# Up projection of a float32 encoder kernel: hi and lo tokens in one 512-column matmul per weight block

## The chip, the core and the metric

The kernel runs on one core of a Trainium2 chip. Engines named here: TensorE (PE in the profile; its weight loads are PEld), VectorE (DVE), ScalarE (ACT), GpSimd (POOL) and SyncE (SP), which issues the transfers. The metric is device time in microseconds (us), the median of several runs; lower is better.

## What is computed

Two layers over 256 tokens of width 2048, all in float32. Each layer is attention with three head groups and then a squared-ReLU MLP. What matters here is the MLP, whose hidden width is 8192:

```python
for l in range(DEPTH):                      # DEPTH = 2
    h = rmsnorm(x, norm1_g[l])
    proj = h @ w_in[l]
    ...                                     # three attention mixers -> mixed
    x = x + mixed @ w_out[l]
    h2 = rmsnorm(x, norm2_g[l])
    x = x + jnp.square(jax.nn.relu(h2 @ w_up[l])) @ w_down[l]
```

## The kernel before

**Three passes for float32.** Every operand of a projection is split in two: `hi`, a copy rounded to the type float32r, and `lo`, the remainder `value - hi`. A product is the sum of three matmuls: hi x hi, hi x lo and lo x hi. The tokens are kept transposed in `xt` (a hi and a lo tensor, each `[128, 16, 256]`: 16 blocks of 128 input features, 256 tokens). Weights arrive as *units* of 256 rows x 512 columns (512 KB) in `raw_ring` (8 slots). ScalarE casts a unit to `w_hi` (`split_hi`, L604), VectorE subtracts for `w_lo` (`split_lo`, L776); both have `AHEAD = 4` slots. So unit s+4 is cast once unit s has been used, and TensorE comes to it three units later.

**Order of the work.** Each engine runs one list of steps, one per unit, written out by hand in `layer_steps`: 72 units of `w_in` (with attention in between), 32 of `w_out`, then the MLP. The MLP alternates an *up stage* of 32 units (4 chunks of 512 hidden columns, 8 units each) and a *down stage* of 32 units (8 chunks, 4 units each), four times per layer, so 8 up stages and 8 down stages in all. Engines meet only at semaphores; every engine works through its list in order.

**Up chunk** (`up_unit`, L447). Weights are stationary and tokens move: for each of the unit's 2 row blocks `j` and 4 column blocks `f`, three matmuls of 256 columns (L460 `w_hi` with `xt` hi, L461 `w_hi` with `xt` lo, L462 `w_lo` with `xt` hi) add into the same half of an accumulator bank of `acc`. Each matmul has a weight load of its own. A chunk takes two whole banks, `acc[2p]` and `acc[2p+1]`, p being the chunk's parity. ScalarE then reads both with a Relu into `mlp_t` (L717), after its `split_hi` of that step, and increments `evicted[p]`; VectorE squares `mlp_t` in the next step (L1018), ScalarE casts the result to `ht` hi (L723), VectorE forms `ht` lo (L1024).

**Down, in and out chunks** (`rows_unit`, L431, with `three_passes`, L419). Here 128 tokens are stationary and 512 weight columns move: L421, L422, L423. Down chunks are read by VectorE (L1009).

**Accumulator banks.** There are eight of 512 float32 columns: `acc` (4), `ps_s` (attention scores and part of the first chunk), `ps_p` (transposed probabilities, the same), `ps_v` (attention values), `ps_t` (transposes). TensorE waits for `evicted[p]` before a chunk's first unit, that is for the reading of the chunk two earlier.

**Around the first up stage.** The second norm's transposed tokens are still being made: TensorE transposes x into `ps_t` (L468) after steps 104 + 1 and 104 + 2, VectorE reads it (L822), ScalarE and VectorE split it (L617, L834), and the units of the first up chunk wait for their block (`panel_done`).

Of the kernel before, what the change touches and what calls it, by code (L numbers as in the profile page):

```python
# [28 lines left out]
P = 128  # L29
# [119 lines left out]
def encoder(nc, x_in, norm1_g, w_in, a_qnorm_g, a_knorm_g, a_rel_bias, b_qnorm_g, b_knorm_g, b_sinks, c_qnorm_g,  # L149
            c_knorm_g, c_lambda_q1, c_lambda_k1, c_lambda_q2, c_lambda_k2, c_subln_g, w_out, norm2_g, w_up, w_down,  # L150
            consts, out):
    with ExitStack() as ctx:
        def sb(name, shape, dt=F32):
            return ctx.enter_context(nc.sbuf_tensor(name, shape, dt))
# [6 lines left out]
        xt = [sb(f"xt_{h}", [P, KT, SEQ], F32R) for h in ("hi", "lo")]  # L161
# [32 lines left out]
        acc = ctx.enter_context(nc.psum_tensor("acc", [P, 4, CW], F32))  # L194
        ps_s = ctx.enter_context(nc.psum_tensor("ps_s", [P, CW], F32))
        ps_p = ctx.enter_context(nc.psum_tensor("ps_p", [P, CW], F32))
        ps_v = ctx.enter_context(nc.psum_tensor("ps_v", [P, CW], F32))
        ps_t = ctx.enter_context(nc.psum_tensor("ps_t", [P, CW], F32))
# [10 lines left out]


# [24 lines left out]
        rstd_ready = sem("rstd_ready")  # L235
        relu2 = sem("relu2")
# [181 lines left out]
        def _(pe):  # L418
# [28 lines left out]
            def up_unit(pl, u, k, chunk):  # L447

                slot, p = u % AHEAD, chunk % 2
                if k == 0:  # L450
                    pe.wait_ge(evicted[p], pl.evictions(chunk))
                unit_is_split(pl, u)
                for j in range(2):
                    for f in range(4):
                        o = acc[:, 2 * p + f // 2, (f % 2) * SEQ:(f % 2 + 1) * SEQ]
                        hi, lo = (w[:, slot, j, f * P:(f + 1) * P] for w in (w_hi, w_lo))
                        kt = 2 * k + j
                        last = k == UPC - 1 and j == 1

                        pe.matmul(o, hi, xt[0][:, kt, :], start=kt == 0 and f % 2 == 0, stop=False, skip_group_check=True)  # L460
                        pe.matmul(o, hi, xt[1][:, kt, :], start=False, stop=False, skip_group_check=True)  # L461
                        mm = pe.matmul(o, lo, xt[0][:, kt, :], start=False, stop=last, skip_group_check=True)  # L462
                mm.then_inc(unit_done, 1)
# [106 lines left out]
            def mlp(pl, s, part, buf, c, k, n):  # L570
                if part == "up":
                    if s < LOOP0 and c == 0:
                        pe.wait_ge(panel_done, pl.at(PANELS, PANELS_BEFORE + FIRST_X2 + k + 1))
                    up_unit(pl, s, k, n)
                else:
                    if k == 0 and c % 4 == 0:

                        done = (4 if s >= DOWN3 else 0) + 2 * (buf + 1) + (8 if s >= DOWN3 else 0)
                        pe.wait_ge(h_done, pl.at(H_CHUNKS, done, 4))
                    rows_unit(pl, s, ht, (8 * buf + 2 * k, 8 * buf + 2 * k + 1), n, k == 0, k == 3, CW)  # L580
                if s in T_USE:
                    use_t(pl, s)
# [17 lines left out]
        def _(act):  # L600
# [112 lines left out]
            def activations(pl, s, part, c, k, n):  # L713

                if part == "up" and k == UPC - 1:
                    act.wait_ge(unit_done, pl.unit(s + 1 + AHEAD))
                    act.activation(mlp_t[c % 2][:, :], acc[:, 2 * (n % 2):2 * (n % 2) + 2, :].rearrange("p b n -> p (b n)"),  # L717
                                   ACT.Relu).then_inc(evicted[n % 2], 1)
# [46 lines left out]
        def _(dve):  # L765
# [228 lines left out]
            def mlp(pl, s, part, buf, c, k, n):  # L994
# [16 lines left out]
                if s == UNITS - 1:  # L1011
                    split_lo(pl, s + AHEAD)
                late = late_chunk(s, part, c, k, 0)
                if late is not None:
# [3 lines left out]
                    dve.tensor_tensor(mlp_t[q % 2][:, :], mlp_t[q % 2][:, :], mlp_t[q % 2][:, :], ALU.mult).then_inc(relu2, 1)  # L1018
# [162 lines left out]
```

## Time and profile before

| | |
|---|---|
| median of 3 runs | 2197.22 us (2193.01 to 2197.33) |
| the profiled execution | 2191.94 us |
| its span, first to last instruction | 2190.1 us |
| mean granted TensorE clock over the span | 0.997 |
| TensorE matmul busy | 98% |
| TensorE weight load busy | 87% |
| VectorE busy | 59% |
| ScalarE busy | 45% |
| GpSimd busy | 9% |

The span is what the trace covers; 1.84 us of the execution lie around it. A matmul's duration in the trace reaches from its start to the end of its passage through the array, so durations of neighbouring matmuls overlap and their sum is more than the time that they take. What one costs in a row of them is the distance from one start to the next.

### The profile page before, as it was taken

To read this page: it belongs to the slowest core of one execution; us is meant where nothing else is said; L and a number is where in the kernel's file an instruction comes from. 1 tells how busy PE (TensorE), PEld (TensorE's weight loads), DVE (VectorE), ACT (ScalarE), POOL (GpSimd) and SP (SyncE) were. 2 spreads that over 40 slices of the span, in tenths; PEclk is the share of its full clock that TensorE was granted. 3 is DMA by queue.
4 is the path that set the end of the run, shared out by engine and by line. 5 is a ranking of instruction groups with operands and counts; after the bars stand their busy time and mean duration, and the time that the engine had idled before them with its cause. 6 is when DMAs were issued, how large, how long until landed. Compare 5 with 4: busy or idle time off the path is not lost.

```text
span 2190.1 us, 31018 instructions
## 1 busy us (share of the span) xinstructions
PE 2154.4 (98%) x12790; PEld 1895.0 (87%) x12790; DVE 1301.6 (59%) x1737; ACT 989.5 (45%) x1357; POOL 196.7 (9%) x170
## 2 busy tenths in 40 slices
PE   8999999999999999999999999999999999999999
PEld 6777888998998998899878777889989989988987
DVE  7778546555556555555677775465555555555556
ACT  5545544443344344344445455444434433443444
POOL 3223230000000000000022322200000000000000
PEclk9999999999999999999999999999999999999999
DMA  8553336656655655665556533466566556556554
GB/s 268 157 177 107 118 132 184 182 184 194 188 185 193 187 184 190 192 183 191 183 163 184 150 97 125 144 176 181 191 193 184 184 194 190 183 192 190 184 187 151
DMA packets 203756, 384.45 MB, mean 176 GB/s; under 512 B 13310, under 2 KB 20192, under 8 KB 203616
## 3 DMA queue, kind: packets, MB, share of 16 engines
q1 hardware_dynamic: 202816, 382.11, 56.1%
q8 instruction: 101, 1.65, 0.3%
q10 hardware_dynamic: 800, 0.37, 0.1%
q14 instruction: 39, 0.32, 0.0%
HBM read 380.31 MB, written 2.12 MB: 175 GB/s over the span
## 4 chain that ended last, share of the span: by engine, by line
PE 91%; DVE 6%; ACT 1%; SPq 1%; issue 0%; DMA 0%; DVEq 0%; ACTq 0%
PE acc L421 17%; PE acc L423 17%; PE acc L422 17%; PE acc L462 11%; PE acc L461 11%; PE acc L460 11%; DVE w_lo L776 3%; PE ps_t L468 2%; PE ps_s L519 1%; PE ps_s L518 1%; PE ps_p L533 1%; PE ps_v L549 1%; PE ps_v L550 1%; ACT w_hi L604 1%; DVE small L795 0%
## 5 line engine op out<-in xcount | busy, mean ns | idle before, releaser
L776 DVE TENSOR_TENSOR w_lo<-raw_ring,w_hi 128x1024 fp32r<-128x1024 f32 (+1 forms) x690 | 851.4, 1235 | 791.1 <-ACT w_hi L604 789.8
L604 ACT CAST w_hi<-raw_ring 128x1024 fp32r<-128x1024 f32 (+1 forms) x724 | 751.6, 1038 | 988.1 <-PE acc L423 567.6
L460 PE MATMUL acc<-xt_hi,w_hi 128*128 128x256 f32 x2048 | 580.6, 283 | 0.0
L462 PE MATMUL acc<-xt_hi,w_lo 128*128 128x256 f32 x2048 | 580.3, 283 | 0.0
L461 PE MATMUL acc<-xt_lo,w_hi 128*128 128x256 f32 x2048 | 580.3, 283 | 0.0
L421 PE MATMUL acc<-w_hi,ht_hi 128*128 128x512 f32 x1280 | 503.2, 393 | 0.0
L423 PE MATMUL acc<-w_hi,ht_lo 128*128 128x512 f32 x1280 | 499.1, 390 | 0.0
L422 PE MATMUL acc<-w_lo,ht_hi 128*128 128x512 f32 x1280 | 498.7, 390 | 0.0
L460 PEld LDWEIGHTS acc<-xt_hi,w_hi 128*128 128x128 f32 x2048 | 393.5, 192 | 0.3
L461 PEld LDWEIGHTS acc<-xt_lo,w_hi 128*128 128x128 f32 x2048 | 393.5, 192 | 0.3
L462 PEld LDWEIGHTS acc<-xt_hi,w_lo 128*128 128x128 f32 x2048 | 393.4, 192 | 0.0
L421 PEld LDWEIGHTS acc<-w_hi,ht_hi 128*128 128x128 f32 x1280 | 240.4, 188 | 52.2 <-issue 3.3
L423 PEld LDWEIGHTS acc<-w_hi,ht_lo 128*128 128x128 f32 x1280 | 240.3, 188 | 50.6
L422 PEld LDWEIGHTS acc<-w_lo,ht_hi 128*128 128x128 f32 x1280 | 240.6, 188 | 48.4
L421 PE MATMUL acc<-w_hi,xt_hi 128*128 128x512 f32 (+1 forms) x512 | 203.0, 397 | 0.0
L423 PE MATMUL acc<-w_hi,xt_lo 128*128 128x512 f32 (+1 forms) x512 | 195.5, 382 | 0.0
L422 PE MATMUL acc<-w_lo,xt_hi 128*128 128x512 f32 (+1 forms) x512 | 194.8, 381 | 0.0
L421 PEld LDWEIGHTS acc<-w_hi,xt_hi 128*128 128x128 f32 x512 | 97.7, 191 | 27.1 <-issue 10.9
L423 PEld LDWEIGHTS acc<-w_hi,xt_lo 128*128 128x128 f32 x512 | 97.5, 191 | 19.1
L422 PEld LDWEIGHTS acc<-w_lo,xt_hi 128*128 128x128 f32 x512 | 97.9, 191 | 15.8
L1125 POOL TENSOR_TENSOR head_sq<-head_in,rope_s 128x256 f32<-128x256 f32 (+1 forms) x20 | 15.0, 752 | 975.9 <-DVE small L857 975.9
L1140 POOL TENSOR_TENSOR w_lo<-raw_ring,w_hi 128x1024 fp32r<-128x1024 f32 x34 | 81.9, 2408 | 214.4 <-ACT w_hi L604 214.4
(141 smaller groups left out, 1372.2 us busy)
## 6 DMA issues: line engine op xcount, KB each, us to landing
raw_ring<-in_w_up_dram SPq DMA_DIRECT2D x256, 512.0 KB, 3.7
raw_ring<-in_w_down_dram SPq DMA_DIRECT2D x256, 512.0 KB, 3.6
raw_ring<-in_w_in_dram SPq DMA_DIRECT2D x132, 512.0 KB, 3.9
raw_ring<-in_w_out_dram SPq DMA_DIRECT2D x64, 512.0 KB, 3.6
raw_ring<-in_w_in_dram SPq DMA_DIRECT2D x16, 256.0 KB, 2.8
x<-in_x_dram SPq DMA_DIRECT2D x4, 512.0 KB, 8.8
out_dram<-x SPq DMA_DIRECT2D x4, 512.0 KB, 3.9
bias_t<-ext_bias SPq DMA_DIRECT2D x2, 512.0 KB, 8.1
```

The source lines that it names most:

```text
L421: pe.matmul(out_ap, t_hi, m_hi, start=start, stop=False, skip_group_check=True)
L422: pe.matmul(out_ap, t_hi, m_lo, start=False, stop=False, skip_group_check=True)
L423: return pe.matmul(out_ap, t_lo, m_hi, start=False, stop=stop, skip_group_check=True)
L460: pe.matmul(o, hi, xt[0][:, kt, :], start=kt == 0 and f % 2 == 0, stop=False, skip_group_check=True)
L461: pe.matmul(o, hi, xt[1][:, kt, :], start=False, stop=False, skip_group_check=True)
L462: mm = pe.matmul(o, lo, xt[0][:, kt, :], start=False, stop=last, skip_group_check=True)
L468: mm = pe.transpose(bank[:, n * P:(n + 1) * P], b, ident)
L518: pe.matmul(ps_s[:, 0:P], q[lo:lo + HD, b, 0:P], k[lo:lo + HD, kb, 0:P], start=True, stop=True)
L519: pe.matmul(ps_s[:, P:3 * P], q[lo:lo + HD, b, P:2 * P], k[lo:lo + HD, kb, :], start=True, stop=True).then_inc(scored, 1)
L604: act.copy(w_hi[:, u % AHEAD, :, 0:cols], raw_ring[:, u % RAWS, :, 0:cols]).then_inc(hi_ready, 1)
L776: dve.tensor_tensor(w_lo[:, u % AHEAD, :, 0:cols], raw_ring[:, u % RAWS, :, 0:cols], w_hi[:, u % AHEAD, :, 0:cols].bitcast(F32), ALU.subtr ...
L1140: pool.tensor_tensor(w_lo[:, u % AHEAD, :, :], raw_ring[:, u % RAWS, :, :], w_hi[:, u % AHEAD, :, :].bitcast(F32), ALU.subtract).then_inc( ...
```

## The change

`xt` hi and lo become two views of one tensor in which, for each feature block, the 256 hi tokens are followed by the 256 lo tokens. `up_unit` sends both as one matmul of 512 columns over `w_hi` into a whole bank, and then the `w_lo` matmul of 256 columns onto the bank's first half. An up chunk so takes four banks (0 to 3 or 4 to 7), the second half of each holding the `w_hi` x lo part. To have eight banks, all the PSUM names become parts of one tensor: `ps_v` 0, `ps_t` 1, `acc` 2 to 5, `ps_s` 6, `ps_p` 7. Four waits are added on TensorE per layer, ahead of the first up chunk (scores and probabilities read) and ahead of the second (values and transposes read). ScalarE copies the four second halves to `mlp_t` (and signals `lo_out`), VectorE adds the four first halves and then signals `evicted`. Relu moves into the squaring: max with 0 and multiply in one instruction.

```diff
-        xt = [sb(f"xt_{h}", [P, KT, SEQ], F32R) for h in ("hi", "lo")]
+        xt_both = sb("xt", [P, KT, 2, SEQ], F32R)
+        xt = [xt_both[:, :, h, :] for h in range(2)]
...
-        acc = ctx.enter_context(nc.psum_tensor("acc", [P, 4, CW], F32))
-        ps_s = ctx.enter_context(nc.psum_tensor("ps_s", [P, CW], F32))
-        ps_p = ctx.enter_context(nc.psum_tensor("ps_p", [P, CW], F32))
-        ps_v = ctx.enter_context(nc.psum_tensor("ps_v", [P, CW], F32))
-        ps_t = ctx.enter_context(nc.psum_tensor("ps_t", [P, CW], F32))
+        psum = ctx.enter_context(nc.psum_tensor("psum", [P, 8, CW], F32))
+        ps_v, ps_t, acc, ps_s, ps_p = psum[:, 0, :], psum[:, 1, :], psum[:, 2:6, :], psum[:, 6, :], psum[:, 7, :]
...
+        def up_banks(n):
+
+            return psum[:, 4 * (n % 2):4 * (n % 2) + 4, :]
...
             def up_unit(pl, u, k, chunk):
 
-                slot, p = u % AHEAD, chunk % 2
+                slot, p, bank = u % AHEAD, chunk % 2, up_banks(chunk)
                 if k == 0:
                     pe.wait_ge(evicted[p], pl.evictions(chunk))
                 unit_is_split(pl, u)
                 for j in range(2):
+                    kt = 2 * k + j
+                    both = xt_both[:, kt, :, :].rearrange("p h q -> p (h q)")
                     for f in range(4):
-                        o = acc[:, 2 * p + f // 2, (f % 2) * SEQ:(f % 2 + 1) * SEQ]
                         hi, lo = (w[:, slot, j, f * P:(f + 1) * P] for w in (w_hi, w_lo))
-                        kt = 2 * k + j
-                        last = k == UPC - 1 and j == 1
-
-                        pe.matmul(o, hi, xt[0][:, kt, :], start=kt == 0 and f % 2 == 0, stop=False, skip_group_check=True)
-                        pe.matmul(o, hi, xt[1][:, kt, :], start=False, stop=False, skip_group_check=True)
-                        mm = pe.matmul(o, lo, xt[0][:, kt, :], start=False, stop=last, skip_group_check=True)
+
+                        pe.matmul(bank[:, f, :], hi, both, start=kt == 0, stop=False, skip_group_check=True)
+                        mm = pe.matmul(bank[:, f, 0:SEQ], lo, xt[0][:, kt, :], start=False, stop=kt == KT - 1, skip_group_check=True)
                 mm.then_inc(unit_done, 1)
...
+                    if s == UP0:
+                        pe.wait_ge(maxed, pl.at(JOBS, JOBS + 1))
+                        pe.wait_ge(pt_copied, pl.at(FILLS, FILLS + 1))
+                    if s == UP0 + UPC:
+                        pe.wait_ge(pv_copied, pl.at(FILLS, FILLS + 1))
+                        pe.wait_ge(t_free, pl.at(T_USES, T_BEFORE + T_NUMBER[OUT_LAST[3] + 3] + 1))
                     up_unit(pl, s, k, n)
...
                 if part == "up" and k == UPC - 1:
                     act.wait_ge(unit_done, pl.unit(s + 1 + AHEAD))
-                    act.activation(mlp_t[c % 2][:, :], acc[:, 2 * (n % 2):2 * (n % 2) + 2, :].rearrange("p b n -> p (b n)"),
-                                   ACT.Relu).then_inc(evicted[n % 2], 1)
+                    act.copy(mlp_t[c % 2][:, :].rearrange("p (f q) -> p f q", f=4), up_banks(n)[:, :, SEQ:2 * SEQ]).then_inc(lo_out, 1)
...
+                if part == "up" and k == UPC - 1:
+                    v = mlp_t[c % 2][:, :].rearrange("p (f q) -> p f q", f=4)
+                    dve.wait_ge(lo_out, pl.at(H_CHUNKS, (c + 1) + (0 if s < LOOP0 else 4), 4))
+                    dve.tensor_tensor(v, up_banks(n)[:, :, 0:SEQ], v, ALU.add).then_inc(evicted[n % 2], 1)
...
                     dve.wait_ge(evicted[m % 2], pl.evictions(m) + 1)
-                    dve.tensor_tensor(mlp_t[q % 2][:, :], mlp_t[q % 2][:, :], mlp_t[q % 2][:, :], ALU.mult).then_inc(relu2, 1)
+                    dve.scalar_tensor_tensor(mlp_t[q % 2][:, :], mlp_t[q % 2][:, :], 0.0, mlp_t[q % 2][:, :], ALU.max,
+                                             ALU.mult).then_inc(relu2, 1)
```

## Rows read from the trace of the kernel before

**Rows 1.** The page: busy us (share of the span) and instructions.

```profile
PE 2154.4 (98%) x12790; PEld 1895.0 (87%) x12790; DVE 1301.6 (59%) x1737; ACT 989.5 (45%) x1357; POOL 196.7 (9%) x170
```

**Rows 2.** The page: the chain that ended last, by engine and line.

```profile
PE 91%; DVE 6%; ACT 1%; SPq 1%; issue 0%; DMA 0%; DVEq 0%; ACTq 0%
PE acc L421 17%; PE acc L423 17%; PE acc L422 17%; PE acc L462 11%; PE acc L461 11%; PE acc L460 11%; DVE w_lo L776 3%; PE ps_t L468 2%; PE ps_s L519 1%; PE ps_s L518 1%; PE ps_p L533 1%; PE ps_v L549 1%; PE ps_v L550 1%; ACT w_hi L604 1%; DVE small L795 0%
```

**Rows 3.** Busy time by stretch: one up stage, then one down stage.

```profile
core 0: us, PE busy (x) PEld busy (x) DVE busy (x) ACT busy (x) POOL busy (x), PEclk, DMA share, GB/s
559.75:651.90 92.15, 92.15 (x769) 92.15 (x768) 47.34 (x40) 39.13 (x38) 0.00 (x0) 1.00 0.62 185
651.90:738.97 87.07, 87.07 (x387) 72.13 (x385) 50.73 (x48) 35.46 (x34) 0.00 (x0) 1.00 0.61 192
```

**Rows 4.** The page, costliest groups: count, busy us, mean ns, idle before.

```profile
L460 PE MATMUL acc<-xt_hi,w_hi 128*128 128x256 f32 x2048 | 580.6, 283 | 0.0
L461 PEld LDWEIGHTS acc<-xt_lo,w_hi 128*128 128x128 f32 x2048 | 393.5, 192 | 0.3
L422 PEld LDWEIGHTS acc<-w_lo,ht_hi 128*128 128x128 f32 x1280 | 240.6, 188 | 48.4
```

**Rows 5.** Timeline of TensorE, end of an up stage: start us, duration us, instruction.

```profile
651.54 0.28 PE L460 MATMUL acc<-xt_hi,w_hi 128*128 128x256 f32 x1
651.66 0.28 PE L461 MATMUL acc<-xt_lo,w_hi 128*128 128x256 f32 x1
651.78 0.28 PE L462 MATMUL acc<-xt_hi,w_lo 128*128 128x256 f32 x1
651.90 0.40 PE L421 MATMUL acc<-w_hi,ht_hi 128*128 128x512 f32 x1
```

**Rows 6.** Timeline of TensorE, end of the next down stage.

```profile
738.52 0.39 PE L422 MATMUL acc<-w_lo,ht_hi 128*128 128x512 f32 x1
738.74 0.39 PE L423 MATMUL acc<-w_hi,ht_lo 128*128 128x512 f32 x1
738.97 0.28 PE L460 MATMUL acc<-xt_hi,w_hi 128*128 128x256 f32 x1
```

**Rows 7.** Waits between 379.64 and 1010 us: us in total, times, longest.

```profile
DVE w_lo L776 <- ACT w_hi L604: 282.7, 223, 1.9
ACT w_hi L604 <- PE acc L462: 202.3, 124, 1.8
ACT w_hi L604 <- PE acc L423: 156.5, 97, 1.7
```

**Rows 8.** Timelines of ScalarE, then of VectorE, behind the chunk ending at 652 us.

```profile
652.16 1.05 ACT L604 CAST w_hi<-raw_ring 128x1024 fp32r<-128x1024 f32 x1 [1.83 <-PE acc L462]
653.11 1.02 ACT L717 ACTIVATE head_sq<-acc 128x1024 f32<-128x1024 f32 x1
654.90 1.05 ACT L604 CAST w_hi<-raw_ring 128x1024 fp32r<-128x1024 f32 x1 [0.77 <-PE acc L423]
...
653.25 1.23 DVE L776 TENSOR_TENSOR w_lo<-raw_ring,w_hi 128x1024 fp32r<-128x1024 f32 x1 [1.67 <-ACT w_hi L604]
655.98 1.23 DVE L776 TENSOR_TENSOR w_lo<-raw_ring,w_hi 128x1024 fp32r<-128x1024 f32 x1 [1.51 <-ACT w_hi L604]
657.13 1.22 DVE L1018 TENSOR_TENSOR head_sq<-head_sq 128x1024 f32<-128x1024 f32 x1
```

**Rows 9.** One line's durations (min/median/max ns), then groups by line and shape.

```profile
L957 DVE TENSOR_TENSOR x<-acc,x x8: 1215/1217/1225, 329.9 to 1467.4; 128x1024 f32<-128x1024 f32 x8
...
L1009 DVE SCALAR_TENSOR_TENSOR x<-acc,rstd,x 128x512 f32<-128x512 f32 x128 | 89.8, 743 | 0.2
...
L670 ACT ACTIVATE probs<-probs,neg_max 128x256 f32<-128x256 f32 x64 | 31.8, 497 | 0.0
```

**Rows 10.** Durations (ns), first to last start (us), of three reading lines.

```profile
L822 DVE TENSOR_TENSOR panel<-ps_t,cur x2: 684/688/692, 387.9 to 394.0; 128x512 f32<-128x512 f32 x2
...
L918 DVE COPY probs_t<-ps_p x28: 544/550/559, 113.9 to 307.2; 128x384 f32<-128x384 f32 x28
...
L686 ACT COPY mixed<-ps_v x28: 252/258/366, 119.4 to 313.4; 128x128 f32<-128x128 f32 x24, 128x256 f32<-128x256 f32 x4
```

**Rows 11.** Granted clock: the whole core, then one attention stretch (columns as Rows 3).

```profile
core 0: 2190.1 us, clock 0.997
...
178.00:190.00 12.00, 9.46 (x37) 6.81 (x35) 10.15 (x40) 4.70 (x16) 2.59 (x2) 0.86 0.35 99
```

More of the change, by code:

```diff
@@ L235, in encoder @@
         rstd_ready = sem("rstd_ready")
+        lo_out = sem("lo_out")
         relu2 = sem("relu2")
```

## The prediction

> **What bounds the kernel now.** I read the page's busy shares first: TensorE works 98% of the span, VectorE 59%, ScalarE 45% [rows 1]. The chain of work that ended last says the same in another way: 91% of it is TensorE, and the three matmul lines of the up projection, L460 to L462, hold a third of it [rows 2]. VectorE's 6% of the chain belongs to the attention part, because in the MLP the waits view shows nobody but helpers waiting: ScalarE for TensorE to free a weight slot, VectorE for ScalarE's cast [rows 7]. No row there has TensorE waiting, neither for an eviction nor for a weight unit, and none has anyone waiting for a transfer. In an up stage TensorE is busy for all of its 92.15 us at full granted clock (1.00, the 2.4 GHz level), with VectorE at 47 us, ScalarE at 39 us and the DMA engines at 0.62 [rows 3]. So an up stage lasts as long as its matmuls take one after another, and only the distance from one start to the next matters there, not the 283 ns that one is in flight [rows 4].
>
> **The price of one matmul.** An up stage has 4 chunks x 8 units x 24 = 768 matmuls of 256 columns: 92.15 / 768 = 120.0 ns each. A down stage has 8 x 4 x 12 = 384 of 512 columns: 87.07 / 384 = 226.7 ns each [rows 3] (the printed counts, 769 and 387, take in a neighbour or two at the edges). Twice the columns cost 106.7 ns more, not 120 more: 0.4167 ns a column, and a fixed 226.7 - 512 x 0.4167 = 13.3 ns for every matmul with its weight load, whatever its length.
>
> **What the change takes away on TensorE.** Before, a weight block costs 3 x 120.0 = 360.0 ns. After, the columns are the same 768, but in two matmuls instead of three: 226.7 + 120.0 = 346.7 ns. The saving is one fixed part, 3 x 119.99 - 226.74 - 119.99 = 13.2 ns. The page counts 2048 such blocks [rows 4] (2 layers x 4 up stages x 32 units x 8), so 2048 x 13.23 = 27.1 us, 3.4 us per up stage. The sum assumes that lengths may alternate without a penalty. The trace has both transitions, one each at every border of the stages: a 256-column matmul followed by a 512-column one starts it 120 ns later (651.78 to 651.90) [rows 5], and a 512-column one followed by 256 columns starts it 230 ns later at two decimals (738.74 to 738.97) [rows 6]. Each has its own 190 ns weight load [rows 4], begun under the matmul before and already overlapping the next one, and the distance is set by the length of the earlier matmul. That is the new inner loop exactly: long, short, long, short. From below, the bound is that the fixed part vanishes in part of the matmuls; from above, that the load of `w_hi` behind a short matmul takes its whole 192 ns. I take 120 and 227, since those rows show just these neighbours.
>
> The Trainium skill, page "TensorE: Matmul & The Clock Gate", section "Wait — 56ns, not 53.3ns?", gives about 2.5 ns as the fixed cost of a warm matmul beyond its columns, and so speaks against most of this gain. By it, an estimate, the change would save 2048 x 2.5 = 5 us. The trace disagrees, with 13.3 ns in a stream where each matmul has a weight load.
>
> **Reading out an up chunk.** Before, ScalarE's Relu (1.02 us) ends the chunk: last matmul starts at 651.78, the cast of the next unit runs from 652.16, Relu from 653.11 to 654.13 [rows 5, 8]. After, ScalarE's copy stands at the same place with the same 1024 elements, but in four runs of 256: 1.02 us at least, and at most four separate instructions of 256, 4 x 0.497 = 1.99 us [rows 9]. I take 1.02, the row of the same engine, bank and count, since it stays one instruction. The new add on VectorE is queued behind `split_lo` of the same step, which ends at 654.48 [rows 8]. It costs 1.22 us by the add of the same size out of PSUM (L957), at most 2 x 0.743 = 1.49 us by L1009 [rows 9]. So it ends near 655.7, about 3.9 us after the last matmul's start, 1.6 us later than Relu's end. What is queued behind it on VectorE is the next `split_lo`, which started at 655.98 only because its cast came then [rows 8]: nothing is late with 1.22 us, and with the upper ends (copy 1.99, add 1.49: ready at 656.6) it is 0.6 us late. Who waits for it: TensorE comes to that unit three units later, some 8 us on, and a split is ready about 2.5 us after its slot is freed. That is a cover of over 5 us. On ScalarE the next cast starts at 654.90, past the copy's 654.13 (with 1.99 us, 0.2 us late, under the same cover).
>
> TensorE itself waits for the add only when it comes back to those banks. After another up chunk that is 8 x 2.77 = 22 us later; after the last chunk of a stage it is one down chunk, 12 matmuls x 4 units x 226.7 ns = 10.9 us later. 3.9 us against 10.9: cost zero. If that cover were gone, every microsecond of delay would be a microsecond of the stage. 32 adds x 1.22 = 39 us more on VectorE lie in 725 us of up stages in which it was half idle [rows 3].
>
> **Squaring with max.** The form with a scalar operand instead of the plain multiply: 1.22 us before [rows 8], between 1.22 and 1.49 after [rows 9]. Its follower, the cast to `ht`, comes one step later, and the down stage reads the last of the chunks 16 units on. Cost zero; nothing waits.
>
> **The four waits per layer.** Those ahead of the first up chunk (379.64 us in layer 0) want scores and probabilities to have been read: last such read starts at 307.2, and the last copy of the values, wanted ahead of the second chunk, at 313.4 [rows 10]. Past by over 60 us. The transposes wanted ahead of the second chunk are read by 394.0 + 0.7 = 394.7 us [rows 10]; the chunk comes after 8 units, at 379.6 + 8 x 2.77 + 0.7 = 402.5 us. 7.8 us to spare. A satisfied wait ahead of a unit (each unit has one) shows no gap in the 120 ns; I allow 0 to 0.1 us for each of the eight, so 0 to 0.8 us, and take 0.
>
> **The rest.** Casting into `xt` with a stride between blocks, and other bank numbers for attention, move nothing in time: same instructions and counts, and each pair of readers keeps its semaphore. Transfers are issued by the progress of the splits; a unit in 2.77 instead of 2.88 us lifts the DMA share from 0.62 to about 0.64 in up stages [rows 3]: not a bound.
>
> **Sum.** 27.1 us off TensorE, 0 added elsewhere. The profiled execution took 2191.94 us with a span of 2190.1; by it the changed kernel has a span of 2163.0 and 2164.8 us. The median of the runs before lies 5.3 us above that execution, and their spread is 4.3 us. Against the median: 2197.2 - 27.1 = **2170.1 us**.
>
> **Rivals.**
>
> *A. The fixed cost stays* (2197 us). The 13.3 ns would belong not to each matmul but to each change of the weights: of the two matmuls over one `w_hi` the second would pay nothing now, and its going would save nothing, so 2197.2 - 0. For this speaks that the block loaded twice is in fact the same. Against it: then L460 to L461 would be closer together than L461 to L462, and both are 120 ns [rows 5]. The page of the Trainium skill named above would put the time between the two, at an estimated 2192 us.
>
> *B. The load of `w_hi` no longer hides* (up to 2317 us, slower). Before, two of three matmuls in a row use `w_hi`; after, the next `w_hi` must be loaded entirely under the short `w_lo` matmul. If that made the short one last as long as its load is recorded, 192 ns instead of 120 [rows 4], the price would be 2048 x 72 = 147 us, less 27 of gain: 2197 + 120 = 2317. It decides as soon as the short matmul's distance passes 120.0 + 13.2 = 133.2 ns. Against it: the load of `w_hi` already follows a `w_lo` matmul (L462 to L460), in 120 ns, and the transition of rows 5 puts a 512-column one behind it in 120 ns too.
>
> *C. The read-out comes late* (2170 to 2250 us). If copy and add took 7 us longer than priced, the first reuse of banks after an up stage would hold TensorE. There are 8 such borders and each microsecond over costs 8 us. It needs the add to end later than 10.9 us; rows give 3.9, 5 at the upper ends.
>
> *D. More goes than one fixed part* (2143 us). If behind a long matmul the swap of weights were hidden, each block would save 2 x 13.2 ns: 54 us. The down stages, all long ones, show 226.7 and so don't hide it [rows 3].
>
> **Chances and range.** The forecast 0.87; A, whole or in part, 0.05; B 0.03; C 0.02, half of it still faster; D 0.03. A measurement of this kernel can tell about 0.2%, 4.4 us, from no change. Faster by more: 0.87 + 0.03 + 0.01 + a fifth of A = 0.92; within: 0.04; slower: 0.04. The range: the runs before spread from 2193.0 to 2197.3, which gives 2165.9 to 2170.2. The granted clock averaged 0.997, so about 7 us of full-speed work were lost in all, in attention stretches such as 178 to 190 us at 0.86 [rows 11]; such a stretch more or less is 2 to 4 us either way. The unknown costs add up to 1 us. 2165.9 - 4 = 2162, 2170.2 + 1 + 4 = 2175, and I round outwards: 2162 to 2176. It leaves out nearly all of the four rivals, 0.13, and some of the forecast's own tail.
>
> **What the profile of after should show.** The new `w_hi` line with 2048 matmuls of 512 columns and the `w_lo` line with 2048 of 256; an up stage of 8 x 4 x 2.773 = 88.7 us in place of 92.15; starts 0.23 and 0.12 apart by turns (B: 0.19 for the short one; A: 0.36 for the pair; D: 0.33). No row with TensorE waiting for VectorE's add, VectorE about 39 us busier, the copy near 1.02 and the add near 1.22 us. Down stages and the attention part unchanged, the clock 1.00 in up stages. The prediction is wrong if the pair of starts isn't 347 ns, or if TensorE shows a gap at the border of up and down.

## The result and the profile after

The changed kernel takes 2180.76 us (median of 4 runs, 2177.23 to 2182.62) against 2196.64 us for the kernel before (one run more than the three above); the ratio is 0.9933, 95% interval 0.9915 to 0.995. It is 15.9 us faster. The forecast was 2170.1 us, 27.1 us faster, with a range that ended at 2176. The sign was right, the gain was forecast 11 us too large, and the measured time lies outside the range.

The page of the changed kernel: busy shares (answers to [rows 1]), then its up projection among the costliest groups (answers to [rows 4]).

```profile
PE 2143.7 (98%) x10742; PEld 1787.6 (82%) x10742; DVE 1338.0 (61%) x1769; ACT 989.8 (45%) x1357; POOL 196.9 (9%) x170
...
L462 PE MATMUL psum<-xt,w_hi 128*128 128x512 f32 x2048 | 722.9, 398 | 0.0
L463 PE MATMUL psum<-xt,w_lo 128*128 128x256 f32 x2048 | 575.0, 281 | 0.0
```

The instructions are those that were foretold: 2048 fewer matmuls, 2048 long and 2048 short ones in the up projection, VectorE 36 us busier (39 were foretold; each add starts 0.09 us before the recorded end of the `split_lo` ahead of it, so their busy times overlap). TensorE is still busy 98% of the time. Busy time by stretch, an up stage and the down stage behind it (answers to [rows 3]):

```profile
core 0: us, PE busy (x) PEld busy (x) DVE busy (x) ACT busy (x) POOL busy (x), PEclk, DMA share, GB/s
562.73:653.17 90.44, 90.44 (x513) 78.47 (x512) 50.76 (x43) 39.20 (x38) 0.00 (x0) 1.00 0.66 187
653.17:740.24 87.07, 87.07 (x387) 72.08 (x385) 51.86 (x49) 35.46 (x34) 0.00 (x0) 1.00 0.66 193
```

Here is the gap. The down stage is what it was, 87.07 us. The up stage fell from 92.15 to 90.44 us, not to the 88.7 of the prediction, with no idle time on TensorE and the granted clock at 1.00. It has 256 pairs of a long and a short matmul: 90.44 / 256 = 353.3 ns a pair, where 346.7 was forecast. The timeline of TensorE shows how the pairs follow each other:

```profile
599.82 0.40 PE L462 MATMUL psum<-xt,w_hi 128*128 128x512 f32 x1
600.06 0.28 PE L463 MATMUL psum<-xt,w_lo 128*128 128x256 f32 x1
600.17 0.40 PE L462 MATMUL psum<-xt,w_hi 128*128 128x512 f32 x1
600.40 0.28 PE L463 MATMUL psum<-xt,w_lo 128*128 128x256 f32 x1
600.52 0.40 PE L462 MATMUL psum<-xt,w_hi 128*128 128x512 f32 x1
600.76 0.28 PE L463 MATMUL psum<-xt,w_lo 128*128 128x256 f32 x1
600.88 0.40 PE L462 MATMUL psum<-xt,w_hi 128*128 128x512 f32 x1
```

Long starts lie 350, 350 and 360 ns apart (599.82, 600.17, 600.52, 600.88), over and over: three pairs in 1060 ns. But one stage of the same execution runs otherwise. The first up stage of the second layer, behind its transposes:

```profile
1484.79 0.39 PE L462 MATMUL psum<-xt,w_hi 128*128 128x512 f32 x1
1485.02 0.28 PE L463 MATMUL psum<-xt,w_lo 128*128 128x256 f32 x1
1485.13 0.39 PE L462 MATMUL psum<-xt,w_hi 128*128 128x512 f32 x1
...
1485.48 0.39 PE L462 MATMUL psum<-xt,w_hi 128*128 128x512 f32 x1
...
1485.83 0.39 PE L462 MATMUL psum<-xt,w_hi 128*128 128x512 f32 x1
```

Three pairs in 1485.83 - 1484.79 = 1040 ns, 346.7 a pair, the forecast sum, for three whole chunks. The parts of the sum are not those of the forecast: at full resolution (the trace has whole nanoseconds) the start behind a long matmul comes 230 ns later and that behind a short one 117, where 227 and 120 were forecast. The same instructions, over the same kinds of operands, have two steady speeds. I call them the fast and the slow rhythm.

Over the eight up stages the starts give 739.0 us before and 723.9 after (six of 90.44, and 91.39 and 89.86 where transposes are mixed in): 15.1 us saved, which is the difference of the medians within a microsecond. The two profiled spans differ by 10.3 us only, since the first up stage of the changed kernel's profiled execution starts 4.6 us later (384.28 us against 379.64), behind a stretch of low granted clock that the kernel before did not have:

```profile
55.00:75.00 20.00, 16.54 (x65) 13.25 (x64) 11.10 (x15) 7.97 (x11) 3.24 (x3) 0.83 0.33 97
...
55.00:75.00 20.00, 16.53 (x77) 13.45 (x76) 13.70 (x18) 9.57 (x12) 4.96 (x6) 1.00 0.38 106
```

(The first line is the changed kernel's, the second that of the kernel before; columns as above, the last but two is the granted clock.) The instructions there are the same but for bank numbers and the place of `xt`, and the mean granted clock differs between executions of one kernel (0.994 to 0.998 in the four of the changed kernel), so I do not put these 4.6 us down to the change.

The read-out of a chunk stands as priced. Timelines of ScalarE, then VectorE, behind the chunk that ends at 653 us (answers to [rows 8]):

```profile
653.43 1.05 ACT L611 CAST w_hi<-raw_ring 128x1024 fp32r<-128x1024 f32 x1 [1.78 <-PE psum L463]
654.38 1.01 ACT L724 COPY head_sq<-psum 128x1024 f32<-128x1024 f32 x1
656.17 1.05 ACT L611 CAST w_hi<-raw_ring 128x1024 fp32r<-128x1024 f32 x1 [0.78 <-PE psum L426]
...
654.51 1.23 DVE L782 TENSOR_TENSOR w_lo<-raw_ring,w_hi 128x1024 fp32r<-128x1024 f32 x1 [1.60 <-ACT w_hi L611]
655.65 1.22 DVE L1022 TENSOR_TENSOR head_sq<-psum,head_sq 128x1024 f32<-128x1024 f32 x1
657.26 1.22 DVE L782 TENSOR_TENSOR w_lo<-raw_ring,w_hi 128x1024 fp32r<-128x1024 f32 x1 [0.39 <-ACT w_hi L611]
658.40 1.22 DVE L1028 SCALAR_TENSOR_TENSOR head_sq<-head_sq 128x1024 f32<-128x1024 f32 x1
```

Copy 1.01, add 1.22, squaring with max 1.22 us; the add ends 3.8 us after the chunk's last matmul started (656.87 against 653.05), and the next `split_lo` still waits 0.39 us for its cast, so the add delays nothing.

### The profile page after: what moved, and what is told of

Its sections match the earlier page's. It is cut to its first block, busy times and chain, and to the rows that moved or that the text cites. A ratio compares the mean times of both kernels' runs of the same rounds, so it can differ in the third digit from the quotient of the medians.

```text
span 2179.8 us, 26958 instructions
## 1 busy us (share of the span) xinstructions
PE 2143.7 (98%) x10742; PEld 1787.6 (82%) x10742; DVE 1338.0 (61%) x1769; ACT 989.8 (45%) x1357; POOL 196.9 (9%) x170
## 4 chain that ended last, share of the span: by engine, by line
PE 91%; DVE 6%; ACT 1%; issue 1%; DMA 0%; SPq 0%; DVEq 0%; ACTq 0%
PE psum L462 22%; PE psum L424 18%; PE psum L426 17%; PE psum L425 17%; PE psum L463 11%; DVE w_lo L782 3%; PE psum L469 2%; PE psum L520 1%; PE psum L519 1%; PE psum L534 1%; PE psum L550 1%; PE psum L551 1%; ACT w_hi L611 1%; DVE small L801 0%; DMA raw_ring<-in_w_in_dram 0%
## 5 line engine op out<-in xcount | busy, mean ns | idle before, releaser
L462 PE MATMUL psum<-xt,w_hi 128*128 128x512 f32 x2048 | 722.9, 398 | 0.0
L463 PE MATMUL psum<-xt,w_lo 128*128 128x256 f32 x2048 | 575.0, 281 | 0.0
L424 PE MATMUL psum<-w_hi,ht_hi 128*128 128x512 f32 x1280 | 502.7, 393 | 0.0
L426 PE MATMUL psum<-w_hi,ht_lo 128*128 128x512 f32 x1280 | 498.6, 390 | 0.0
L425 PE MATMUL psum<-w_lo,ht_hi 128*128 128x512 f32 x1280 | 498.2, 389 | 0.0
L462 PEld LDWEIGHTS psum<-xt,w_hi 128*128 128x128 f32 x2048 | 384.6, 188 | 94.5
L463 PEld LDWEIGHTS psum<-xt,w_lo 128*128 128x128 f32 x2048 | 386.9, 189 | 0.3
L424 PEld LDWEIGHTS psum<-w_hi,ht_hi 128*128 128x128 f32 x1280 | 240.3, 188 | 52.5 <-issue 3.3
L425 PEld LDWEIGHTS psum<-w_lo,ht_hi 128*128 128x128 f32 x1280 | 240.4, 188 | 48.5
L424 PE MATMUL psum<-w_hi,xt 128*128 128x512 f32 (+1 forms) x576 | 230.6, 400 | 0.0
L426 PE MATMUL psum<-w_hi,xt 128*128 128x512 f32 (+1 forms) x576 | 221.9, 385 | 0.0
```

What stands on the lines that cost most here:

```text
L424: pe.matmul(out_ap, t_hi, m_hi, start=start, stop=False, skip_group_check=True)
L425: pe.matmul(out_ap, t_hi, m_lo, start=False, stop=False, skip_group_check=True)
L426: return pe.matmul(out_ap, t_lo, m_hi, start=False, stop=stop, skip_group_check=True)
L462: pe.matmul(bank[:, f, :], hi, both, start=kt == 0, stop=False, skip_group_check=True)
L463: mm = pe.matmul(bank[:, f, 0:SEQ], lo, xt[0][:, kt, :], start=False, stop=kt == KT - 1, skip_group_check=True)
```

## The experiments

Theory P, formed on the profile after: an alternating stream of long and short matmuls has two rhythms, and how it is entered decides between them. Its rivals: the read-out or the new banks cost the missing time (E), the accumulator does (A), the joined token tile is slow as an operand (T, called R in the expectation of e2), the place in the program fixes the speed (F). Up stages below are taken from the starts in the traces, in one profiled execution of each kernel; a stage without transposes is meant unless said. Ratios are against the kernel before, run beside each experiment. Single rows of a stretch have the columns of [rows 3].

### e1: the changed kernel again

> The changed kernel once more, as the reference of this set. In its profile a pair (long w_hi matmul, short w_lo matmul) took 353.3 ns in 31 of the 32 chunks' worth of steady stretches seen, and 346.7 ns in three chunks of the second layer's first up stage. Theory P (two steady rhythms of an alternating stream; which one a stretch falls into depends on how it is entered): 353 in most stages again, perhaps with another stage at 347; about 2181 us. Theory F (a fixed property of each stage's data or addresses): the very same three chunks at 347 and no others.

Measured: 2179.12 us, ratio 0.9929 (0.9914 to 0.9944). The six up stages without transposes took 90.440 us each, as before. Both stages with transposes (one per layer) now ran at 346.7 ns a pair from the fifth unit on, in the first layer too, where the first profiled execution had 353. F in its strict form falls: the same instructions at the same place took either speed in two executions. The stages that follow a down stage directly were slow in all twelve cases of the two executions. (The expectation counts 31 slow chunks of 32; with three at 346.7 ns a pair it is 29, one of which changes to the fast rhythm behind its transposes.)

### e3: the change without the merged matmul

```diff
-                        pe.matmul(bank[:, f, :], hi, both, start=kt == 0, ...)
+                        pe.matmul(bank[:, f, 0:SEQ], hi, xt[0][:, kt, :], start=kt == 0, ...)
+                        pe.matmul(bank[:, f, SEQ:2 * SEQ], hi, xt[1][:, kt, :], start=False, ...)
                         mm = pe.matmul(bank[:, f, 0:SEQ], lo, xt[0][:, kt, :], ...)
```

> The change without its merged matmul: new tile, new banks, copy and add, max in the squaring, the four waits, but w_hi moves hi and lo tokens in two 256-column matmuls again, into the two halves of the bank. If the read-out and the waits cost nothing: 120.0 ns a matmul, up stage 92.15 us, 2197 us, no change against the kernel before. Rival E (the read-out or the new banks eat the missing 12 us): 2205 to 2209 us and up stages of 93.6 us.

Measured: 2193.37 us, ratio 0.9998 (0.9989 to 1.0008). The stage from 563.26 us:

```profile
563.26:655.41 92.15, 92.15 (x770) 92.15 (x768) 50.74 (x43) 39.12 (x38) 0.00 (x0) 1.00 0.63 184
```

92.15 us, 120.0 ns a matmul, with the new tile, banks, copy, add and waits; the eight up stages add up to 739.0 us, as in the kernel before. All that side of the change costs nothing that can be measured (the interval leaves room for 2 us in the whole kernel): E falls, and the prediction's zeros stand. What is missing is lost between matmuls.

### e4: the short matmul into the second half of the bank

```diff
-                        mm = pe.matmul(bank[:, f, 0:SEQ], lo, xt[0][:, kt, :], ...)
+                        mm = pe.matmul(bank[:, f, SEQ:2 * SEQ], lo, xt[0][:, kt, :], ...)
```

> The short matmul adds onto columns 256 to 511 of its bank in place of 0 to 255 (the sum of both halves is the same). Theory P: nothing changes, pair of 353 ns, 2181 us. Rival A (the accumulator: a second write to the same columns so soon after the first must wait): the distance between the two writes of a column changes by 107 ns, so the pair should move, to 347 or up to 360 and more; 2168 to 2195 us.

Measured: 2176.7 us, ratio 0.992 (0.9902 to 0.9937), up stages 90.440 us, within a nanosecond of the changed kernel's. All eight add up to 723.9 us, as in the first execution of the changed kernel, so the 2.4 us between the medians of e4 and e1 do not come from them (the profiled executions had mean granted clocks of 0.998 and 0.995). A falls: which half of the bank is added to again plays no part in the pair.

### e6: all up matmuls long

```diff
-                        mm = pe.matmul(bank[:, f, 0:SEQ], lo, xt[0][:, kt, :], ...)
+                        mm = pe.matmul(bank[:, f, :], lo, both, ...)
```

> The short matmul is made long: w_lo too moves hi and lo tokens (the extra product lo x lo is added, which the other kernels leave out). All up matmuls have 512 columns now, out of the joined tile, over the same weights. Theory P: no change of length, so 226.7 ns each and up stages of 512 x 226.7 = 116.1 us. Rival T (the operands are slow in themselves): 233 to 236 ns, 119.3 to 120.8 us.

Measured: 2384.66 us (one execution). The stage from 588.07 us:

```profile
588.07:704.12 116.05, 116.05 (x513) 96.13 (x512) 50.75 (x43) 39.14 (x38) 0.00 (x0) 1.00 0.52 146
```

116.05 / 512 = 226.7 ns: the price of the down stages, out of the joined tile and into whole banks. T falls. With one length alone, long or short, a matmul costs its columns and 13.3 ns; the loss needs both.

### e8: the kernel before, its down stages alternating

```diff
+                if cols == CW and u >= LOOP0:
+                    ...
+                            pe.matmul(o[:, 0:CW], t_hi, w_hi[:, slot, j, 0:CW], ...)
+                            pe.matmul(o[:, 0:SEQ], t_lo, w_hi[:, slot, j, 0:SEQ], ...)
+                            pe.matmul(o[:, 0:CW], t_hi, w_lo[:, slot, j, 0:CW], ...)
+                            mm = pe.matmul(o[:, SEQ:CW], t_lo, w_hi[:, slot, j, SEQ:CW], ...)
+                    ...
+                    return
```

> The kernel before, its up projection untouched; in the down stages the 512-column w_hi x lo pass is cut into two of 256 columns, in the order long, short, long, short. Nothing of the change is in it. Theory P (taking turns is the cause, whatever the operands): a block of four takes more than the sum of its parts, 2 x 226.7 + 2 x 120 = 693.5 ns; in the slow rhythm 2 x 353.3 = 706.6, a down stage of 90.4 us. Rival T (it is the up stage's operands): 693.5 ns, a down stage of 88.8 us.

Measured: 2212.94 us (one execution). Three down stages in turn (256 pairs each):

```profile
473.27:563.72 90.45, 90.45 (x515) 78.44 (x513) 50.74 (x48) 35.54 (x34) 0.00 (x0) 1.00 0.60 186
655.88:744.64 88.76, 88.76 (x514) 78.26 (x513) 50.74 (x48) 35.55 (x34) 0.00 (x0) 1.00 0.61 189
836.79:927.24 90.45, 90.45 (x515) 78.41 (x513) 50.74 (x48) 35.54 (x34) 0.00 (x0) 1.00 0.60 186
```

Nothing of the change is in this kernel, stationary and moving operands have changed places, and yet the two values return: 90.45 / 256 = 353.3 and 88.76 / 256 = 346.7 ns a pair. This is the strongest support for P: it is alternation itself. Each of these stages keeps its rhythm from end to end. Of all eight down stages four were entered slow and four fast, by turns, and the distance at the border told which: where the first long matmul started 120 ns after the last short one of the up stage, the stage was slow; where it started 124 or 125 ns after, it was fast. No transpose stands at these borders.

### e2 and e5: long ones and short ones in groups

e2 sends the four long matmuls of a row block and then its four short ones; e5 the eight long ones of a unit and then its eight short ones. The edit of e5 (e2 has both `f` loops inside one `j` loop):

```diff
                 for j in range(2):
                     ...
                     for f in range(4):
+                        pe.matmul(bank[:, f, :], w_hi[:, slot, j, f * P:(f + 1) * P], both, ...)
+                for j in range(2):
+                    for f in range(4):
+                        mm = pe.matmul(bank[:, f, 0:SEQ], w_lo[:, slot, j, f * P:(f + 1) * P], xt[0][:, 2 * k + j, :], ...)
```

> The four long matmuls of a row block first, then its four short ones. Theory P (the 6.6 ns per block arise from long and short ones taking turns): long after long 226.7, short after short 120, at most 2 changes of length per 8 matmuls, so an up stage of 256 x 346.7 = 88.75 us if a change costs nothing, and 88.75 + 0.4 us if each pair of changes costs the 6.6 ns of before; kernel about 2197 - 27 = 2170 us. Rival R (the 512-column matmul out of the joined tile, or into the whole bank, costs 233 to 236 wherever it stands): up stage 90.4 us as in the changed kernel, 2181 us.

> Per unit the eight long matmuls first, then the eight short ones: one change of length per 8 matmuls. Grouped by four, a long one behind a long one took 233.7 ns where the down stages show 226.7, and an up stage 89.79 us. Theory P (each change of length upsets the stream for a few matmuls, as behind small matmuls in the attention part of the kernel before, where 512-column starts lie 236, 233, 235, 224 ns apart and come down to 227 after a dozen): the surplus over 88.75 us halves again, up stage 89.2 to 89.4 us, kernel 2170 us. Rival T (the joined token tile as moving operand is slow in itself): long ones at 233.7 throughout, 16 x 7 = 56 ns in 32 units more per 8... up stage 90.2 us or above, 2180 us.

Measured: e2 2174.36 us, ratio 0.9907 (0.9892 to 0.9923); e5 2173.41 us, ratio 0.9903 (0.9886 to 0.9919). A stage of e2, then one of e5:

```profile
562.19:651.98 89.79, 89.79 (x514) 78.48 (x513) 50.76 (x43) 39.18 (x38) 0.00 (x0) 1.00 0.68 188
...
560.17:649.53 89.36, 89.36 (x513) 78.66 (x512) 50.75 (x43) 39.34 (x38) 0.00 (x0) 1.00 0.67 189
```

Over 256 x 346.7 = 88.75 us the surplus is 1.69 us alternating, 1.04 in groups of four, 0.61 in groups of eight. It shrinks with the number of changes of length, but not in proportion: 512, 128 and 64 changes a stage give 3.3, 8.1 and 9.5 ns a change. My expectation of 88.75 to 89.15 us for e2 failed: a long matmul behind a long one took 233.7 ns there (mean of 1536) and 230.7 in e5 (mean of 1792), not 226.7. For e5 the stage came as expected (89.2 to 89.4 us). Both kernels missed the 2170 us expected of them, by 4.4 and 3.4 us. A change of length upsets the spacing of several matmuls behind it, not only its own. The kernel before has this too, in the attention part, behind small matmuls:

```profile
242.72 0.40 PE L422 MATMUL acc<-w_lo,xt_hi 128*128 128x512 f32 x1
242.96 0.40 PE L423 MATMUL acc<-w_hi,xt_lo 128*128 128x512 f32 x1
243.19 0.40 PE L421 MATMUL acc<-w_hi,xt_hi 128*128 128x512 f32 x1
243.43 0.39 PE L422 MATMUL acc<-w_lo,xt_hi 128*128 128x512 f32 x1
243.65 0.39 PE L423 MATMUL acc<-w_hi,xt_lo 128*128 128x512 f32 x1
```

Long starts 240, 230, 240 and 220 ns apart (235, 233, 235, 225 at full resolution), where the down stages keep 227.

The same stands at every border of an up stage and a down stage before, right behind the last line of [rows 5]:

```profile
651.90 0.40 PE L421 MATMUL acc<-w_hi,ht_hi 128*128 128x512 f32 x1
652.14 0.40 PE L422 MATMUL acc<-w_lo,ht_hi 128*128 128x512 f32 x1
652.37 0.39 PE L423 MATMUL acc<-w_hi,ht_lo 128*128 128x512 f32 x1
652.60 0.40 PE L421 MATMUL acc<-w_hi,ht_hi 128*128 128x512 f32 x1
```

At full resolution the long matmuls behind the last short one start 233, 235, 229, 232 and 231 ns apart before they settle at about 227. At each of the eight borders the first five distances together are 27 to 29 ns over five times 226.7.

### e7: transposes ahead of the chunks

A *kick* below is a transpose that is sent only to disturb the stream; the *entry* of a stage is the change from the matmuls ahead of it to its own.

```diff
                 unit_is_split(pl, u)
+                if k == 0:
+                    for n in range(q + 1):
+                        pe.transpose(bank[:, 0, 0:P], x[:, 0, 0:P], ident)
```

> The changed kernel with c + 1 transposes of 128 columns ahead of chunk c of every up stage, into a bank that the chunk then clears (only to disturb the stream; 2.5 per chunk x 0.12 us = 10 us of extra work in all). Theory P (which rhythm the stream falls into depends on how it is entered): of the 32 chunks some take 64 x 346.7 = 22.19 us behind their kick and others 22.61 us, by the number of transposes perhaps. Theory F (the rhythm belongs to the place): 353.3 ns a pair everywhere but in the chunks that had 347 before.

Measured: 2178.55 us (one execution) with 80 transposes added. The fast rhythm held in 21 of 32 chunks: behind one transpose in 8 of 8, behind two in 8 of 8, behind three in 3 of 8, behind four in 2 of 8. One stage was fast in all its chunks and took 89.84 us with its ten transposes, some 0.108 us each over 88.75. So the entry matters, as P says, and chunks of the same instructions at other places differ. The number of transposes isn't separated from the rhythm ahead of them: the two fast chunks behind four transposes both follow a fast chunk behind three.

### e9, e12 and e11: kicks to choose the rhythm

The edit of e9 and e11; e12 has `k == 0 and q == 0` alone:

```diff
+                if k == 0 and (q == 0 or u == UP0 + UPC):
+                    pe.transpose(bank[:, 0, 0:P], x[:, 0, 0:P], ident)
```

> The changed kernel with one transpose of 128 columns ahead of each up stage's first chunk, and one more ahead of the second chunk of a layer's first up stage (behind the transposes that this stage has anyway); the bank is cleared by the chunk behind it. With 1 to 4 transposes ahead of the chunks, a chunk behind one transpose ran at 346.6 ns a pair in all eight stages. If a rhythm, once entered, lasts to the stage's end: 256 x 346.6 + 0.11 us = 88.85 us for a stage in place of 90.44, 8 x 1.6 = 13 us off the changed kernel: 2166 us. If chunk borders or waits throw it back: between 2166 and 2179 us, with some chunks at 353.5.

> One transpose ahead of each up stage and no other. In e9 the first stage of layer 0 was in the fast rhythm (346.6 ns a pair) behind its own transposes and was thrown into the slow one (353.3) by the second kick. If the rhythm holds until something disturbs the stream: all 32 chunks at 346.7, six stages of 88.83 us and two of 89.8 us (0.9 us for the transposes that they have anyway), 712.7 us in all against 714.2 with the second kick and 723.9 in the changed kernel; 2170 us. If the rhythm drifts by itself: some later chunk at 353.3.

> Grouped by eight, with the same kicks. Without kicks its up stages took 89.36 us, 0.61 over 256 x 346.7. If grouping has a fast rhythm as well that an entry selects: 88.85 us, 2169 us or less. If its surplus is paid at every change of length whatever the entry: 89.36 + 0.11 = 89.5 us, 2174 us.

Measured: e9 2171.58 us, ratio 0.9908 (0.9893 to 0.9923); its six stages behind down stages took 88.83 to 88.84 us from their first long matmul (the kick starts 0.03 us ahead of it), the forecast to 0.02 us:

```profile
563.86:652.69 88.83, 88.83 (x514) 77.67 (x513) 50.77 (x43) 39.27 (x38) 0.00 (x0) 1.00 0.65 191
```

The kernel missed its forecast of 2166 us by 5.6. The second kick of layer 0 threw that stage from 346.6 into 353.5, the one of layer 1 did not.

e12, without that second kick, has a median of 2170.93 us, ratio 0.9905 (0.9888 to 0.9921). That is near the 2170 expected, by luck, since its profile missed what I had expected. Two of its stages, with the same instructions:

```profile
734.61:825.14 90.53, 90.53 (x514) 78.61 (x513) 50.74 (x43) 39.21 (x38) 0.00 (x0) 1.00 0.65 186
912.24:1001.08 88.84, 88.84 (x515) 77.69 (x513) 50.77 (x43) 39.29 (x38) 0.00 (x0) 1.00 0.66 190
```

Three of its eight stages were slow from end to end (90.53 us), five fast. A transpose ahead of a stage makes the fast rhythm likely, not certain. A stage was fast behind such a kick in 8 of 8 entries in e7, 8 of 8 in e9 and 5 of 8 in e12; without one, entered from a down stage, in 0 of 18 (two executions of the changed kernel, and e4) and in 0 of 6 in e10. What told the 24 entries with a kick apart is when the kick started after the last long matmul of the stage ahead: 230 or 231 ns in the three entries that gave 353 ns a pair, 232 to 238 ns in the 21 that gave 347. With the 120 and 124 ns at the borders of e8, a first start that comes late by a few nanoseconds goes with the fast rhythm. This was read from the traces afterwards; no run tests it, and what delays the start is not shown. No stage changed its rhythm except behind transposes.

e11 (2172.41 us, ratio 0.9914, 0.9895 to 0.9932) kept 89.47 us with its kick, 89.36 + 0.11: in groups the surplus is paid whatever the entry, as its expectation had it (89.5 us; its 2174 us was 1.6 us too high).

### e10: the short one first

```diff
-                        pe.matmul(bank[:, f, :], hi, both, start=kt == 0, ...)
-                        mm = pe.matmul(bank[:, f, 0:SEQ], lo, xt[0][:, kt, :], start=False, ...)
+                        pe.matmul(bank[:, f, 0:SEQ], lo, xt[0][:, kt, :], start=kt == 0, ...)
+                        mm = pe.matmul(bank[:, f, :], hi, both, start=False, ...)
```

> The w_lo matmul of each block ahead of its w_hi matmul: the same alternation, entered with a short one behind the down stage's long ones. Theory P: the sum of a pair is again one of 346.7 or 353.3 ns in each stage, so up stages of 88.75 or 90.44 us and nothing between; which one isn't foretold. 2166 to 2180 us. Against P: any third value held through a stage.

Measured: 2176.58 us, ratio 0.9926 (0.9905 to 0.9947). Six stages of 90.45 us, and the other two, which have transposes of their own, ran at 346.7 ns a pair behind them: the two known values and no third.

## Why the prediction was right or wrong

**The bound: right.** TensorE stayed at 98%, and the waits view shows none of its matmuls waiting in the first layer's up and down stages (384 to 1008 us).

**The price of a matmul: right for streams of one length.** 226.7 and 120.0 ns came back in e6 and e3 with the new operands and banks. A fixed part of 13.3 ns with each matmul is real there.

**The step that failed** is "the sum assumes that lengths may alternate without a penalty". I read it off single transitions at the stage borders ([rows 5, 6]), one long or short matmul behind a whole stage of the other kind, and took 120 and 227 "since those rows show just these neighbours". They show the two neighbours, not the stream. What a change of length costs isn't in the distance across it but in those behind it: past the 120 ns of [rows 5] the trace of before has 233, 235, 229, 232 and 231 ns between long matmuls (shown under e2 and e5), some 27 ns at each border that the reading stopped short of. Kept up, the alternation settles in one of two rhythms, and in 7 of 8 stages of the profiled execution it was the slow one. The mis-sized term is the pair: 353.3 ns in place of 346.7. 2048 x (360.0 - 353.3) = 13.7 us, and with the fast chunks of the second layer 15.1 us, stood against 27.1. The mechanism, one fixed part less for each weight block, was right; what remains of a pair beyond its columns is 33.3 ns and not 2 x 13.3, which gave back half of the gain. All of the loss stands behind the long matmul: in the stage from 562.73 us the next start comes 236.6 ns after a long one, not 226.7, and 116.7 ns after a short one, not 120. Where the fast rhythm was brought about (e9), six up stages took 88.83 us, so the forecast price of a pair exists. The 27 us as a whole were seen in no kernel: e9 took 20.7 us and e12 21.7 us off the medians of the kernel before in their sets (2192.23 and 2192.67 us), each with one or more stages in the slow rhythm.

**The range: too narrow.** I named "the fixed part vanishes in part of the matmuls" as the lower bound and a fully exposed weight load as the upper, gave the second 0.03, and then built the range from the spread of the runs, as if the 346.7 were certain. No case lay between 0 and 27 us of gain but rival A. The trace of before had the hint twice: 512-column starts 235 ns apart behind small matmuls in the attention part, and the same behind every up stage (shown under e2 and e5).

**The zeros: right.** Copy, add, squaring, four waits, bank numbers, stride: e3 measures them together at a ratio of 0.9998 (0.9989 to 1.0008). The add was foretold at 1.22 us and to end 3.9 us after the last matmul's start; it took 1.22 and ended 3.8 us after. (The up stages before are 739 us long in all, not the 725 that the working sets against VectorE's adds; nothing hangs on it.)

**The rivals.** A (nothing, or by the Trainium skill's page "TensorE: Matmul & The Clock Gate", section "Wait — 56ns, not 53.3ns?", an estimated 5 us): the measured gain lies between it and the forecast, but not by its mechanism. In the kernel before and in e3 the second matmul over one `w_hi` costs what the one over a new block does: the starts lie 120.1 and 120.0 ns apart, with 13.3 ns in each. The page's 2.5 ns agree with no stream here. B did not happen: the start behind a short matmul came 111 to 121 ns later in the alternating up stages, never near 192. C and D did not happen; D's 333 ns a pair was seen nowhere.

**Beyond both kernels.** Side by side on one chip e2 ran at 2172.75 to 2175.85 us and the changed kernel at 2177.45 to 2180.73: 4.8 us between the medians, with no overlap. But e4, whose up stages are those of the changed kernel, ran there at 2174.71 to 2180.16, so 2.4 us of such a distance can come from elsewhere; in up stages e2 has 720.2 us against 723.9. e5, e9 and e12 have ratios of 0.9903 to 0.9908 against the kernel before; their intervals overlap that of the changed kernel, so that they beat it rests on their up stages (716.8, 714.2 and 717.8 us in all against 723.9 and, in e1, 722.3), one profiled execution each, not on the ratio. Of them e5 is the one that I would keep: it needs no extra work, and its stages don't depend on the entry.

**What stays open** is what makes the two rhythms. The cause is narrowed to the alternation of lengths, with banks, operands, read-out and order in the pair excluded. What in TensorE's passage from one matmul to the next takes the extra 20 ns in three pairs, and what made the kick of e12 start a few nanoseconds earlier in its three slow stages, no run here tells.

## What to carry to other kernels

Fewer, longer matmuls over one loaded block save the fixed part of each matmul that goes, but price the stream as it will run, not from single transitions: mixed lengths cost 3 to 10 ns at each change here, save in the fast rhythm, and it shows in the distances behind a change, not in the one across it. Where lengths must mix, put the long ones together and the short ones together: groups of eight had a third of the surplus of single turns. If a forecast rests on a spacing that the trace doesn't show in a steady stream, let the range take in half of the gain.

## What the runs showed of the hardware that was not expected

- A steady alternation of 512- and 256-column matmuls, each with its own weight load, at a granted clock of 1.00, runs at 346.7 or at 353.3 ns a pair, in repeating patterns of distances (fast: 230 and 117 ns, or 231, 112, 233 and 117; slow: 232, 118, 240, 120, 236 and 114), and stays there for a whole stage of 256 pairs. The same program took either in different stages (e8, e12) and at the same place in different executions (the changed kernel and e1).
- With a transpose of 128 columns ahead of it, at 0.11 us, a stage was fast in 21 of 24 entries; without one, behind a down stage, in 0 of 24 (in e8, where up and down stages change places, in 4 of 8). The kick started 232 to 238 ns after the matmul ahead of it where 347 ns a pair followed, 230 or 231 where 353 followed.
- After a change of length the distances of several matmuls behind it are off: in groups of four a long one behind a long one takes 233.7 ns, in groups of eight 230.7, in a stream of its own 226.7.
- ScalarE's copy of 256 columns out of each of four banks, in one instruction, took 1.01 us, no more than its Relu over two whole banks (1.02), and VectorE's multiply with max took the 1.22 us of the plain multiply.
